# The last two token blocks computed together, with block products in place of the full gate/up product

## The reference

```
u = rms_norm(h) ; z = u @ w_in                       # 1024 x 2560: q, k, v, a, b
att = band attention over the last 576 keys, 8 heads of 64
cv  = silu(layer_norm(causal depthwise conv, width 31, of a * sigmoid(b)))
h = h + concat(att, cv) @ w_out                      # 1024 x 1024
u = rms_norm(h) ; gate, up = split(u @ w_gate_up)    # 1024 x 5632
h = h + (silu(gate) * up) @ w_down                   # 2816 x 1024
y = h + sigmoid(rms_norm(h) @ w_ple_gate) * (p @ w_ple_proj)
```

## Time and profile before

| | us |
|---|---|
| runs, median (lowest, highest) | 2672.75 (2672.6, 2674.95) |
| the profiled execution, its span from first to last instruction | 2670.6 |
| PE busy | 2661.8 |
| DVE busy | 1585.8 |
| ACT busy | 1153.9 |
| POOL busy | 116.6 |
| DMA queue of SP, 653.31 MB | 71.2% of 16 engines |

### The profile page before, as it was taken

How to read it: one execution, slowest core, us unless ns; L and a number is a source line. 1 busy time by engine, 2 the same in 40 slices (tenths; PEclk the granted TensorE clock), 3 DMA queues, 4 the chain that set the end, 5 groups by cost and what they waited for, 6 DMA issues and landing times.

```text
span 2670.6 us, 39289 instructions
## 1 busy us (share of the span) xinstructions
PE 2661.8 (100%) x14768; PEld 2612.7 (98%) x14768; DVE 1585.8 (59%) x3010; ACT 1153.9 (43%) x1974; POOL 116.6 (4%) x89
## 2 busy tenths in 40 slices
PE   9999999999999999999999999999999999999999
PEld 8999999999999999999999999999999999999999
DVE  4555478988978777755455555554566664431323
ACT  5444367877763233443233443234432234432333
POOL 6222300000000000000000000000000000000000
PEclk9999999999999999999999999999999999999999
DMA  5667798888577877876766767666867676766675
GB/s 198 210 215 241 254 358 273 268 272 277 171 256 233 271 221 242 256 277 242 259 229 238 271 243 250 247 241 224 273 249 251 241 249 238 248 240 240 221 252 183
DMA packets 260744, 655.82 MB, mean 246 GB/s; under 512 B 30380, under 2 KB 143916, under 8 KB 260012
## 3 DMA queue, kind: packets, MB, share of 16 engines
q1 hardware_dynamic: 260556, 653.31, 71.2%
HBM read 528.31 MB, written 126.94 MB: 245 GB/s over the span
## 4 chain that ended last, share of the span: by engine, by line
PE 94%; DVE 2%; DMA 2%; SPq 1%; ACT 1%; issue 1%; POOL 0%; DVEq 0%; POOLq 0%; ACTq 0%
PE psum L191 84%; PE psum L1502 3%; PE psum L1478 2%; PE psum L1466 1%; PE psum L1465 1%; DMA a_cr<-in_cache 1%; DVE ul L678 1%; POOL wres L621 0%; DMA rstd<-in_w_in 0%; PE psum L1495 0%; PE psum L2124 0%; PE psum L2128 0%; PE psum L811 0%; PE psum L810 0%; DVE a_room L708 0%
## 5 line engine op out<-in xcount | busy, mean ns | idle before, releaser
L191 PE MATMUL psum<-uh,wres 128*128 128x416 f32 x5600 | 1569.6, 354 | 2.7 <-DVE wres L1276 1.7
L191 PEld LDWEIGHTS psum<-uh,wres 128*128 128x128 f32 x5600 | 1047.6, 188 | 14.9 <-DVE wres L1276 1.9
L191 PE MATMUL psum<-ul,wres 128*128 128x416 f32 x2800 | 978.1, 349 | 0.0
L1801 ACT ACTIVATE wres<-x 128x1024 fp32r<-128x1024 f32 (+2 forms) x378 | 435.0, 1151 | 1172.2 <-PE psum L191 1156.8
L191 PE MATMUL psum<-wres 128*128 128x416 f32 x3520 | 683.1, 351 | 0.0
L191 PEld LDWEIGHTS psum<-wres 128*128 128x128 f32 x3520 | 658.0, 188 | 8.2 <-issue 2.9
L191 PEld LDWEIGHTS psum<-ul,wres 128*128 128x128 f32 x2800 | 526.6, 188 | 9.0 <-issue 1.3
L1952 DVE SCALAR_TENSOR_TENSOR y<-c_gw,vec,y 128x416 f32<-128x416 f32 (+1 forms) x600 | 295.9, 558 | 2.1
L2070 DVE TENSOR_TENSOR z<-psum,z 128x416 f32<-128x416 f32 x80 | 47.3, 591 | 201.1 <-PE psum L191 201.0
L2060 DVE TENSOR_TENSOR c_up<-psum,c_rstd 128x416 f32<-128x416 f32 x110 | 65.0, 591 | 161.5 <-PE psum L191 161.4
L2046 DVE TENSOR_TENSOR c_g<-psum,c_rstd 128x416 f32<-128x416 f32 x110 | 64.8, 589 | 112.4 <-PE psum L191 111.9
(11 more groups left out here) (192 smaller groups left out, 2258.6 us busy)
## 6 DMA issues: line engine op xcount, KB each, us to landing
x<-in_w_gu SPq DMA_DIRECT2D x220, 512.0 KB, 3.6
wres<-w_gu_lo SPq DMA_DIRECT2D x176, 512.0 KB, 4.3
x<-in_w_down SPq DMA_DIRECT2D x80, 704.0 KB, 4.3
wres<-w_down_lo SPq DMA_DIRECT2D x64, 704.0 KB, 5.5
x<-in_w_ple SPq DMA_DIRECT2D x40, 640.0 KB, 4.6
w_gu_lo<-wres SPq DMA_DIRECT2D x44, 512.0 KB, 5.0
x<-in_w_in SPq DMA_DIRECT2D x40, 512.0 KB, 5.8
x<-in_w_out SPq DMA_DIRECT2D x40, 512.0 KB, 4.4
```

The source lines that it names most:

```text
L191: mm = nc.tensor.matmul(out, w[wp](kw), u[up](ku), start=first and n == 0 and j == 0, stop=last and n == len(kts) - 1 and j == 2)
L1801: nc.scalar.activation(whi[v % 2][:, 0:kts, :], raw[v % 2][:, 0:kts, :], ACT.Copy).then_inc(hi_done, 1)
```

## The change

Blocks 0, 1 and 2 go through `finish` as before. The fourth place in the list is now block 4 (`TURN`), and only its X, Y and O units. Then a new function, `last_pair`, takes block 3 and block 4 together through a list of smaller pieces (`pair_pieces`): the output projection of block 3 (16 pieces O of 4 input tiles, 12 matmuls), then gate and up of both blocks for the 22 hidden tiles, the down product, and the last gate.

Gate and up of two blocks are a product of a 2 x 2 matrix of weights (gate, up by upper and lower half of the 1024 input channels) and a 2 x 2 matrix of activations (halves of the channels by block). In place of its eight block products there are seven, P1 to P7, of sums of blocks (Strassen's scheme in Winograd's form), each of 4 input tiles and 12 matmuls, 22 times. The sums of activations (t1 to t4) are made by VectorE at the opening of the products; because blocks are added, the norm is applied to the activations first. Of the weights' sums there are four (for P3, P5, P6, P7); their high and low parts are made when they are used, those of P1, P2 and P4 come from DRAM as before. The results are combined partly in PSUM (P6, P5, P3 add to what P1 left, P4 to P7; ScalarE copies out the state between) and partly by VectorE.

The down product of the pair stands behind every fourth tile for the first 16 tiles (D, both blocks, 24 matmuls), and at the end for the last six per block (A for block 4, B for block 3, pieces of 12 and 6). Then G and E: last gate and product with p. There are 282 pieces; raw weights have three places, high and low four each.

The sums of weights are made by POOL (`weight_sums`), and SP loads and stores for them in steps, one behind each of the units 40 to 171 of `finish` (`sums_step`), which is from the second half of block 0 into the first half of block 2. They are stored in DRAM (`w_s`).

The convolutions are planned by `tap_plan`: 1 in block 0 as before, 2 from the last P units of block 0 to the first half of block 1, 3 from the end of its second half over the P units into the first units of block 2, 4 in block 2. Norm and swish of 2 and 3 stand at U units. The result of convolution 3 is stored with the mixture of the attention in DRAM and loaded by the pair. The places in SBUF are laid out anew; `project` and `attend` compute what they did.

```diff
+SINGLE, FIRST, SECOND = 3, 4, 3
+TURN = (0, 1, 2, FIRST)
...
+OPENING = ("P1 0", "P2 0", "P1 1", "P2 1", "P1 2", "P2 2", "P1 3", "P2 3", "P6 0", "P6 1", "P5 0", "P5 1", "P3 0", "P3 1",
+           "P7 0", "P6 2", "P4 0", "P5 2", "P7 1", "P6 3", "P4 1", "P3 2", "P5 3", "P7 2", "P3 3", "P4 2")
+def pair_pieces():
+    def product(op, j):
+        return {"op": op, "j": j, "kts": KH, "summed": op in ("P3", "P5", "P6", "P7")}
+    def down(op, m, n):
+        return {"op": op, "m": m, "c": n, "kts": KH if n < 5 else KF - 5 * KH, "summed": False}
+    us = [{"op": "O", "m": m, "h": h, "kts": KH, "summed": False} for m in range(KD) for h in range(2)]
+    us += [product(e[:2], int(e[3:])) for e in OPENING]
+    for j in range(4, KF):
+        us += [product(op, j - (op in ("P7", "P4"))) for op in ("P1", "P7", "P6", "P2", "P5", "P4", "P3")]
+        if j in (4, 8, 12, 16):
+            us += [down("D", m, j // 4 - 1) for m in range(KD)]
+    last = KF - 1
+    us += [product("P7", last), down("A", 0, 4), product("P4", last), down("A", 1, 4), down("A", 2, 4)]
+    us += [down("A", m, 5) for m in range(3)] + [down("A", m, n) for m in range(3, KD) for n in (4, 5)]
+    us += [down("B", m, n) for m in range(KD) for n in (4, 5)]
+    for e in range(2):
+        for m in range(KD):
+            us += [{"op": "G", "e": e, "m": m, "h": h, "kts": KH, "summed": False} for h in range(2)]
+            us.append({"op": "E", "e": e, "m": m, "kts": KP, "summed": False})
+    return us
+def sums_step(sp, t, c, s, i):
+    j, step = divmod(i, 6)
+    b0, b1 = sum_places(c)
+    came, made, kept = c["piece_in"], c["piece_lo"], c["piece_out"]
+    def load(dst, up, h):
+        r = 2 * j + up
+        sp.dma_start(dst, t["w_gu"][r * P:(r + 1) * P, h * KH * P:(h + 1) * KH * P]).then_inc(came, 16)
+    def store(n, src):
+        sp.wait_ge(made, SUM_MADE + 4 * j + {0: 1, 1: 2, 3: 3, 2: 4}[n])
+        sp.dma_start(s["w_s"][(4 * j + n) * P:(4 * j + n + 1) * P, :], src).then_inc(kept, 16)
+    if step == 0:
+        sp.wait_ge(kept, SUM_OUT + 64 * j)
+        load(b0, 1, 0)
+        load(b1, 1, 1)
+    elif step == 1:
+        store(0, b1)
+        load(b0, 0, 0)
+    elif step == 2:
+        store(1, b1)
+        load(b0, 0, 1)
+    elif step == 3:
+        store(3, b0)
+    elif step == 4:
+        sp.wait_ge(kept, SUM_OUT + 64 * j + 48)
+        load(b1, 0, 0)
+        load(b0, 1, 0)
+    else:
+        store(2, b0)
+def weight_sums(nc, c):
+    b0, b1 = sum_places(c)
+    came, made, kept = c["piece_in"], c["piece_lo"], c["piece_out"]
+    @c["block"].gpsimd
+    def _(pool):
+        for j in range(KF):
+            pool.wait_ge(came, SUM_IN + 96 * j + 32)
+            nc.gpsimd.tensor_tensor(b1, b0, b1, ALU.add).then_inc(made, 1)
+            pool.wait_ge(came, SUM_IN + 96 * j + 48)
+            pool.wait_ge(kept, SUM_OUT + 64 * j + 16)
+            nc.gpsimd.tensor_tensor(b1, b1, b0, ALU.subtract).then_inc(made, 1)
+            pool.wait_ge(came, SUM_IN + 96 * j + 64)
+            pool.wait_ge(made, SUM_MADE + 4 * j + 2)
+            nc.gpsimd.tensor_tensor(b0, b0, b1, ALU.subtract).then_inc(made, 1)
+            pool.wait_ge(came, SUM_IN + 96 * j + 96)
+            nc.gpsimd.tensor_tensor(b0, b0, b1, ALU.subtract).then_inc(made, 1)
...
+        def raw_load(n):
+            if n >= NP:
+                return
+            u = us[n]
+            if n >= 3:
+                sp.wait_ge(hi_done, H + n - 2)
+                if n - 3 in low_made_at:
+                    sp.wait_ge(lo_done, L + low_made_at[n - 3])
+            if u["summed"]:
+                sp.wait_ge(c["piece_out"], f["sums"])
+            q = (n + 2) % 3
+            sp.dma_start(f["raw"][q][:, 0:u["kts"] * P], piece_rows(t, s, u)).then_inc(w_in[q], 16)
+        def low_load(n):
+            if n >= NP or us[n]["summed"]:
+                return
+            u = us[n]
+            sp.wait_ge(used, U + n - 3)
+            sp.dma_start(f["lo"][slot(n)][:, 0:u["kts"] * P].bitcast(F32), piece_rows(s, s, u)).then_inc(low_dma[slot(n)], 16)
...
+        sp.wait_ge(f["tap"], f["taps"])
+        raw_load(0)
+        for q in range(2):
+            sp.wait_ge(stored[q], 16 * YB // 2)
+        sp.wait_ge(c["mix_out"][0], f["mix_staged"])
+        for e, src in enumerate((s["mh"], s["ml"])):
+            sp.dma_start(hx[:, e * KD:(e + 1) * KD, :].bitcast(F32),
+                         src.rearrange("(k p) n -> p k n", p=P)[:, :, SECOND * N:(SECOND + 1) * N]).then_inc(mix_in, 16)
+        sp.wait_ge(hi_done, H)
+        raw_load(1)
+        raw_load(2)
+        for m in range(KD):
+            sp.dma_start(hb[:, m, :], t["x"][SECOND * P:(SECOND + 1) * P, m * N:(m + 1) * N]).then_inc(x_in[m], 16)
+        for n in range(4):
+            low_load(n)
+        for n in range(3, 6):
+            raw_load(n)
+        for n, u in enumerate(us):
+            low_load(n + 4)
+            raw_load(n + 6)
...
+        def second_sums(i):
+            if 2 <= i <= 5:
+                k = i - 2
+                scaled(b12r[k], hb, k, V_GFFN, sb, 1)
+                scaled(b22r[k], hb, k + KH, V_GFFN, sb, 1)
+                less(t1r[k], b12r[k], uar[k], ("ub", k))
+                less(t2r[k], b22r[k], t1r[k], ("t1", k))
+            if 3 <= i <= 6:
+                u_low("t2", i - 3, t2l[i - 3], t2r[i - 3], t2h[i - 3])
+            if i == 6:
+                for k in K4:
+                    u_low("t1", k, t1l[k], t1r[k], t1h[k])
+            if i in (7, 8):
+                for k in (2 * i - 14, 2 * i - 13):
+                    less(t3r[k], b12r[k], b22r[k], ("ub4", k))
+                for k in (2 * i - 14, 2 * i - 13):
+                    u_low("b22", k, b22l[k], b22r[k], b22h[k])
+            if i == 9:
+                for k in K4:
+                    u_low("t3", k, t3l[k], t3r[k], t3h[k])
+            if i == 10:
+                for k in K4:
+                    less(t4r[k], uar[KH + k], t2r[k], ("t2", k))
+            if i == 11:
+                for k in K4:
+                    u_low("t4", k, t4l[k], t4r[k], t4h[k])
...
+            elif op in ("P6", "P5", "P3"):
+                pe.wait_ge(kept, kept_at[{"P6": "P1", "P5": "P6", "P3": "P5"}[op], j])
+                mm = product(bank(bank_a(j)), w, RIGHT[op], False, True,
+                             lows({"P6": "t2", "P5": "t1", "P3": "b22"}[op]) if j == 0 else None, True)
+            elif op == "P7":
+                evicted(*(("ua", j - 1) if j else ("ga", 3)))
+                mm = product(bank(3), w, RIGHT[op], True, True, lows("t3") if j == 0 else None)
+            elif op == "P4":
+                evicted("ub", j)
+                mm = product(bank(3), w, RIGHT[op], False, True, lows("t4") if j == 0 else None, True)
...
+        tap_plan = {
+            1: spread(30, places("U", 0) + places("D", 0) + places("U", 0, 1)),
+            2: spread(3, places("P", 0, which=(5, 6, 7))) + spread(15, places("U", 1)) + spread(12, places("D", 1)),
+            3: spread(2, places("U", 1, 1, (10,))) + spread(11, places("D", 1, 1)) + spread(11, places("P", 1)) + spread(
+                6, out_units),
+            4: spread(2, places("U", 2, 0, (10,))) + spread(12, places("D", 2)) + spread(16, places("U", 2, 1)),
+        }
+        taps_of = {v: [(n, r) for n in tap_plan for r, (w, _) in enumerate(tap_plan[n]) if w == v] for v in range(NU)}
...
+                if 0 <= v - SUMS_FROM < 6 * KF:
+                    sums_step(sp, t, c, s, v - SUMS_FROM)
```

More of the change, by code:

```diff
@@ new lines, in piece_high, with sum_places @@
+def piece_high(nc, act, c, f, n):
+    u = f["pieces"][n]
+    q = (n + 2) % 3
+    act.wait_ge(c["w_in"][q], f["W"][q] + 16 * (n // 3 + 1))
+    if n >= 4:
+        act.wait_ge(c["used"], f["U"] + n - 3)
+    cols = slice(0, u["kts"] * P)
+    nc.scalar.activation(f["hi"][n % 4][:, cols], f["raw"][q][:, cols], ACT.Copy).then_inc(c["hi_done"], 1)
+SUM_IN, SUM_MADE, SUM_OUT = 16 * 16, 16, 16 * 16
+def sum_places(c):
+    first = 24 * N + 4 * KH * P
+    return [c["top"][:, first + e * KH * P:first + (e + 1) * KH * P] for e in range(2)]
@@ L1588, in block_units @@
             us += [{"kind": "D", "b": b, "half": half, "m": m} for m in range(KD)]
[L1589 to L1591 removed]
+        us += [{"kind": "P", "b": b, "m": 0}, {"kind": "X", "b": b + 1, "pair": 0}]
         return us + [{"kind": "P", "b": b, "m": m} for m in range(1, KD)]
[L1594 removed]
+    units = [u for b in range(SINGLE + 1) for u in block_units(b)]
     NU = len(units)
@@ L1696, in sig_count, with places @@
             return b * (KF + KD) + (KF if kind == "P" else 0) + n
-        def tap_at(u):
-            if u["b"] + 1 == NB or u["kind"] not in "UD" or (u["kind"] == "D" and u["half"]):
-                return None
-            return u["f"] + u["half"] * (HF + KD) if u["kind"] == "U" else HF + u["m"]
+        def places(kind, b, half=0, which=None):
+            return [v for v, u in enumerate(units) if u["kind"] == kind and u["b"] == b and u.get("half", 0) == half
```

(16 more changed lines are left out.)

731 lines of the change are left out of this document (636 added, 95 removed).

## The result

The changed kernel takes **2710.64 us** (median of 4 runs, 2707.41 to 2714.91) against 2673.0 before (2672.6 to 2674.95): ratio 1.014, 95% interval 1.0127 to 1.0152. It is **slower by 38 us**; 2642 was forecast, and the range ended at 2664. Its profiled span is 2707.5 us, 36.9 over the span of before.

What follows compares the result with a forecast made beforehand. TensorE alone was taken to bound the kernel, at 188.7 ns per matmul. -49.8 + 5 + 6 + 2 + 6 = -30.8 us took 2670.6 to 2639.8, the median 2642, range 2626 to 2664.

Steps and rivals of the forecast that it cites:

- Part 1: Gate and up of the pair: 1848 matmuls for 2112, 264 fewer at 188.7 ns, -49.8 us, the whole gain.
- Parts 2 to 4: TensorE waits in the pair: entry +5 us, opening of the seven products +6, end of the pair +2.
- Part 5: Weight sums beside blocks 0 to 2, in SP's queue and on POOL: +6 us, range 0 to 25.
- Rival (b): SP's queue with the sum chain at 36 us, TensorE waiting 85 us for weights: slower than before, 2721; chance 0.08.
- The chain of one group: Loads, POOL sums and stores of one group of weight sums: 28.0 us, 29 with POOL starts delayed by VectorE.
- SP falls back by some 2 us per group in gate/up: SP's queue beside blocks 0 to 2: some 2 us late per gate/up group, 7 per half block, caught up in between.
- the slack of 8 us: Raw weights in block 1 have 8 us of slack, so blocks 1 and 2 hide SP's lateness.
- It decides at about 32.2 us per group: Chain length per group of weight sums at which the waits in gate/up eat the 37 us of gain left.
- rival (a): Sum chain somewhat longer, 31 us: the weight sums cost 22 us instead of 6, time 2658; chance 0.13.
- latencies rise with load: Argument for the 36 us chain: DMA busy was up to 0.89 at 307 GB/s; no size given.
- DMA carries 328 GB/s: Traffic in gate/up, 384 GB/s beside the last gate, against 345: 5 us late per block, inside the slack.
- Part 6: Convolutions moved on VectorE, block 1 near 70% busy: cost 0, or 5 us in all without the banks' cover.

Runs made afterwards that it cites:

- the half groups' trace: Changed kernel with the same weight sums in half groups of 256 columns in four places, loads, waits and stores spread over three units: 2662.8 us.
- that of the ends: Changed kernel with two orders of SP's queue changed: low loads ahead of x loads at the pair's entry, y stores a piece later at its end: 2692.8 us.
- the last kernel: The kernel of half groups every fourth unit, plus the two changed orders of SP's queue at the pair's entry and end: 2641.0 us, 0.988 of before.
- the kernel of half groups every fourth unit: Changed kernel with sums in half groups in four places, begun every fourth unit from unit 38, none in block 2's seven Y and O units: 2648.2 us.

## Why the prediction was wrong

**Part 1** was right to the matmul. **Parts 2 to 4** had the right places and releasers (TensorE idle once at the entry, once by VectorE in the opening, once after the first E) and cost 23.3 for 13. The entry's DMA moved 381 GB/s where 345 was assumed, and TensorE still stood 5.9 us; the opening's idle was 3.2 for 6, the end's 2.0 for 2. To each came what I had not costed, a lower granted clock behind the idle (below). A side figure of part 2 is off too: 7.2 MB at 229 GB/s make it +16, not +11.

**Part 5 is the step that failed**, with 59.4 us measured for 6. Rival (b)'s outcome is what happened, SP's queue paced by the chain of the sums and a kernel slower than before, but not by its chain of 36 us. Piece by piece:
- "The chain of one group ... 29" held where nothing disturbs it: groups are 28.7 to 30.3 us apart in block 1's gate/up. Its terms were off both ways: a 256 KB load of the sums took 4.7 and not 3.0 (the page's 4.3 also counts the pair's loads), the store 2.4 and not 3.2. That they made up for each other is luck.
- "SP falls back by some 2 us per group in gate/up, 7 in a half block, **and catches up in between**" failed in its last four words. Six down units last 37.4 us and six of the last gate 34, and I set the chain of 29 against these sums. But the groups were 38.1 to 39.5 apart from the second down stretch of block 0 to the output units behind it, where their units alone take 34 to 35, and 33.8 and 38.8 over the first down stretch of block 1; the down stretches lost another 0.1 to 2 us each. Next to nothing was caught up. The likely reason, which no run isolates: a step is issued once per unit, behind that unit's weights, and the loads there stand behind transfers of 704 KB that land 6.3 to 7.3 us after issue in this stretch. And the Y and O units, seven in a row between two blocks, have 24 matmuls as gate and up have; I counted 12.7 groups as exposed, and there were more.
- So the slack of 8 us was spent once, not once per half block: block 0's second gate/up half lost 12.5 us, its last gate 10.0, the output units 4, block 1's halves 8.5 and 7.5, the output units of block 2 10 (there with VectorE's part). Each half of block 1 shows about the 7 us of falling back that I had foreseen, with nothing hidden.
- Rival (b)'s figures seem to fit: "It decides at about 32.2 us per group", and 33.2 was measured. That is partly chance. The 32.2 is meant against units of 27.2 us, and there the groups were 28.7 to 33.6 apart, nearer to rival (a)'s 31; the mean of 33.2 holds the down and last-gate groups, in which both rivals saw no loss. Rival (b)'s price for the sums was 85 for a chain of 36, and 59.4 came. What both lacked is the loss outside gate/up and the slack that doesn't come back. The sentence for them, that "latencies rise with load", was in the prediction: in the stretch from 900 to 1700 raw weights took 3.7 us to land before and 4.9 after.
- "DMA carries 328 GB/s ... inside the slack" was right in kind: putting the saved bytes back cost 3.8 us. (The 0.9 MB in part 5's last sentence would be 1.2 MB per block by its own figures.)
- POOL beside VectorE was put into block 0 with 2 us. It costs 7.5 by itself, in block 2's output units for the most part.

**Part 6** cost 1 to 2 us alone, inside its 0 to 5. What it hid was the coupling: four taps in each output unit of block 2 turn a VectorE loop with room into one of 4.69 us against 4.53, and there POOL's sums come out in full. The moved taps were nearly free alone. That POOL would be without them is likely, as it cost about 1 us ahead of those units, but no run has POOL's sums with the taps where they were.

With the main cause taken away the change gives 2648, and with the ends reordered as well 2641. That this is near the forecast of 2642 is in part chance: in the last trace the entry cost 1.6 us for 5 and the opening 9.7 for 6, and the forecast knew nothing of the reordered ends.

## What to carry to other kernels

A queue that issues both a chain with waits and somebody's weights runs at the chain's pace wherever that is the slower one. Compare them step by step, the longer of step and unit each time, not sum against sum, and count on catching up only where a row shows it. The cure costs no work: more and smaller places, so that every wait is for something issued two units earlier. And before calling an added operation hidden, work out the period of the loop it enters: above 100% of the unit nothing is ever caught up, and the next small disturbance comes out in full.

## What the runs showed of the hardware beyond what I expected

TensorE's granted clock often fell behind short idles. In the half groups' trace (the idle of 4.67 us is in the first window), and in that of the ends, opening of the seven products (an idle of 3.3 us):
```profile
1570.00:1575.00 5.00, 0.52 (x2) 0.51 (x3) 4.22 (x7) 1.87 (x3) 1.90 (x2) 0.88 0.91 294
1575.00:1580.00 5.00, 5.00 (x14) 4.12 (x13) 4.21 (x6) 3.97 (x4) 0.00 (x0) 0.50 0.39 127
1580.00:1585.00 5.00, 5.00 (x27) 4.93 (x26) 4.16 (x5) 1.88 (x3) 1.12 (x2) 0.94 0.52 188
```
```profile
2070.00:2075.00 5.00, 4.45 (x13) 4.28 (x14) 3.10 (x6) 3.00 (x5) 0.00 (x0) 0.50 0.35 108
```
0.50 is the lower level, 1.2 GHz: 14 matmuls in 5 us where 27 run at full clock, so some 2.4 us on top of the idle. In the last kernel an idle of 1.35 us (3.65 busy of 5, at 1945 above) was followed by 1.00. The three idles of after's pair (5.9, 3.2, 2.0 us) each had 0.62 to 0.71 behind or around them. The length of an idle alone does not decide: 2.0 us before the first E had 0.68 behind it in after and 1.00 in the kernel of half groups every fourth unit, and the last kernel's 3.0 us at 1565 had 1.00. Nor is the price fixed: the idle of 3.3 us in the opening, the same in every kernel with the pair, had 3 to 6 us of lower clock around or behind it. So a wait of 3 us can cost up to 3 us more than its length, and the same wait does not always cost the same.

The sums' 256 KB stores, issued one at a time, landed 2.4 us after issue (median), the 128 KB ones, issued four at a time, after 4.8. Which of size and number makes the difference no run shows.
